# Two-block transformer kernel on one core: key tiles that hold two heads, turned queries on all partitions, four bias buffers, first scores ahead of the last values, weights ahead of the norm

## The reference, cut to what matters

```
h = rmsnorm(x) ; qa, ka, va, c_q, c_kv, k_r = split(h @ w_in)
ya = dilated attention, 8 heads of 64, with a distance bias and a mask
q  = rmsnorm(c_q) @ w_uq      -> 8 heads of 64 plain + 32 turned (rope)
kv = rmsnorm(c_kv) @ w_ukv    -> 8 heads of 64 key + 64 value; k_r turned, shared
yb = softmax((q_nope k_nope + q_rope k_rope) * 96**-0.5) @ v
x  = x + rmsnorm([rmsnorm(ya), rmsnorm(yb)] @ w_o) * norm_mix_post
x  = x + rmsnorm(conv_ffn(rmsnorm(x))) * norm_ffn_post
```

## Time and profile before

| | |
|---|---|
| median of 3 runs | 1662.87 us (1662.8 to 1668.37) |
| the profiled execution's own time | 1661.71 us |
| its span, first to last instruction | 1659.9 us |
| mean granted TensorE clock | 0.998 |
| busy: PE, DVE, ACT, POOL | 97%, 74%, 54%, 3% |
| the mixer of the first block, and its output projection | 0 to 152 us of the span |
| scores of `nat` to its first output product | 722 to 758 us |

### The profile page before, as it was taken

The page is one execution under the profiler, slowest core; times in us unless marked ns, Lnnn a source line. Parts: engine busy times, 40 slices in busy tenths (PEclk is TensorE's granted clock), DMA queues, the critical chain, the costliest instruction groups (busy, mean ns, idle before and its releaser), DMA issues.

```text
span 1659.9 us, 28581 instructions
## 1 busy us (share of the span) xinstructions
PE 1617.5 (97%) x10582; PEld 1465.1 (88%) x10582; DVE 1235.2 (74%) x1840; ACT 889.1 (54%) x1153; POOL 42.6 (3%) x54
## 2 busy tenths in 40 slices
PE   8989999999999999999999999999999999999998
PEld 7878999978799999878999999877999997899997
DVE  5765877777788777875877777447687787878787
ACT  5475545465655455565645464544554556665453
POOL 0001000000000000000000014000000000000000
PEclk9999999999999999999999999999999999999999
DMA  7252554544364544431554545543555454345543
GB/s 284 97 196 101 205 199 167 192 155 184 108 248 177 202 175 158 175 127 52 190 198 169 191 162 203 203 152 110 191 193 201 164 191 178 106 174 185 195 177 126
DMA packets 41697, 284.65 MB, mean 171 GB/s; under 512 B 4928, under 2 KB 5056, under 8 KB 8736
## 3 DMA queue, kind: packets, MB, share of 16 engines
q1 hardware_dynamic: 39424, 274.43, 45.2%
q0 software_dynamic: 2208, 9.32, 1.6%
HBM read 282.68 MB, written 1.05 MB: 171 GB/s over the span
## 4 chain that ended last, share of the span: by engine, by line
PE 84%; DVE 9%; ACT 3%; issue 3%; DMA 1%; DVEq 0%; SPq 0%; ACTq 0%
PE bank L1751 14%; PE bank L1753 14%; PE bank L1752 14%; PE bank L1845 8%; PE bank L1846 8%; PE bank L1847 8%; PE bank L1797 4%; PE bank L1798 4%; PE bank L1799 4%; DVE w_lo L982 2%; DVE arena L1249 1%; ACT w_hi L547 1%; PE bank L1733 1%; PE bank L1894 1%; PE bank L2140 1%
## 5 line engine op out<-in xcount | busy, mean ns | idle before, releaser
L1751 PE MATMUL bank<-h_hi,w_hi 128*128 128x256 f32 (+1 forms) x2240 | 642.2, 287 | 11.3 <-DVE w_lo L982 6.3
L1752 PE MATMUL bank<-h_hi,w_lo 128*128 128x256 f32 (+1 forms) x2240 | 636.3, 284 | 0.0
L1753 PE MATMUL bank<-h_lo,w_hi 128*128 128x256 f32 (+1 forms) x2240 | 636.3, 284 | 0.0
L1751 PEld LDWEIGHTS bank<-h_hi,w_hi 128*128 128x128 f32 x2240 | 429.4, 192 | 20.1 <-issue 9.5
L1752 PEld LDWEIGHTS bank<-h_hi,w_lo 128*128 128x128 f32 x2240 | 429.5, 192 | 4.5 <-issue 1.4
L1753 PEld LDWEIGHTS bank<-h_lo,w_hi 128*128 128x128 f32 x2240 | 429.5, 192 | 1.0
L982 DVE TENSOR_TENSOR w_lo<-raw,w_hi 128x2048 fp32r<-128x2048 f32 (+3 forms) x115 | 244.9, 2132 | 115.1 <-ACT w_hi L547 114.8
L1276 DVE TENSOR_TENSOR w_lo<-raw,w_hi 128x2048 fp32r<-128x2048 f32 x145 | 327.5, 2285 | 1.6 <-ACT w_hi L743 1.6
L731 ACT ACTIVATE arena<-arena,par 128x256 f32<-128x256 f32 x220 | 120.4, 594 | 358.9 <-DVE arena L1235 355.7
L743 ACT ACTIVATE w_hi<-raw 128x2048 fp32r<-128x2048 f32 x150 | 286.1, 1907 | 19.8 <-PE bank L1847 19.7
L547 ACT ACTIVATE w_hi<-raw 128x2048 fp32r<-128x2048 f32 (+2 forms) x110 | 194.3, 1772 | 107.4 <-PE bank L1847 39.0
(11 more groups left out here) (193 smaller groups left out, 1288.4 us busy)
## 6 DMA issues: line engine op xcount, KB each, us to landing
raw<-wstream SPq DMA_DIRECT2D x254, 1024.0 KB, 4.8
arena<-window_bias POOLq DMA_DIRECT2D x4, 768.0 KB, 6.7
arena<-dilated_bias POOLq DMA_DIRECT2D x8, 256.0 KB, 3.4
arena<-conv_rows POOLq DMA_DIRECT2D x2, 1024.0 KB, 4.9
raw<-wstream SPq DMA_DIRECT2D x4, 384.0 KB, 3.5
raw<-wstream SPq DMA_DIRECT2D x6, 256.0 KB, 3.0
x<-x_in SPq DMA_DIRECT2D x1, 1024.0 KB, 5.0
raw<-wstream SPq DMA_DIRECT2D x2, 512.0 KB, 7.2
```

Source lines behind the costliest of these rows:

```text
L1751: nc.tensor.matmul(dst, w_parts[0], x_parts[0], start=start, stop=False, **kw)
L1752: nc.tensor.matmul(dst, w_parts[1], x_parts[0], start=False, stop=False, **kw)
L1753: return nc.tensor.matmul(dst, w_parts[0], x_parts[1], start=False, stop=stop, **kw)
```

## The change

Nine things are changed:

- **Front.** `w_hi` of chunk 5 is made one step earlier, ahead of the root and the norm of the queries.
- **Queries and keys of `yb`.** Two chunks of turned rows come first (four heads a tile, cosine rows in one tile, swapped rows in the other), and DVE multiplies them on all 128 partitions, with tables that are repeated four times; four sums on 32 partitions each put them into place. Then come two chunks of plain queries and two of keys, a tile holding two heads, each copied by ACT in four pieces of 64 x 256. There are two chunks fewer.
- **Bias buffers.** Four in place of two (two lie in `lat`, once that is read).
- **First scores.** The scores of heads 0 and 1 are made before the last two value chunks, in `mix` and in `nat`.
- **Values.** Their last two chunks go to banks of their own; ACT copies the second half after exp(1), and PE waits for that copy before S(2,3).
- **Halves in `mix`.** ACT's at 3 and 5, 7 and 9, 10 and 12; DVE's at 5 and 6, 9 and 10, 12 and 14.
- **Halves in `nat`.** Chunk 13 is now split in attention too: ACT's halves at 2 and 3, DVE's at 3 and 4. Chunk 14: ACT's at 5 and 7, DVE's at 8 and 9.
- **`post`.** `piece * gain` first, without the root, three of four pieces beside or ahead of the root; then one instruction does `(piece * gain) * root + x`.
- **`keep_busy`** has 24 transposes in place of 36.

```
-        return [CH] * 9 + [2 * 3 * P] * 4 + [2 * 2 * P] * 4 + [2 * 256] * 2 + [CH] * 4
+        return [CH] * 9 + [2 * 3 * P] * 4 + [2 * 2 * P] * 2 + [2 * 256] * 2 + [CH] * 4
...
+                        if h == 2:
+                            pool.wait_ge(hlo_done, DT + 5)
+                        if h >= 4:
+                            pool.wait_ge(biased, bias_count(h - 4))
+                        pool.dma_start(bias_slot(h), bias_in[:, h * 512:(h + 1) * 512]).then_inc(bias_full[h % 4], 16)
...
+                    if n == 1:
+                        second_values()
...
+                            split_hi(c0 + 5)
                             inv_sqrt()
                             split_h(range(8, 11))
...
-                        2: lambda: half_hi_of(c0 + 19, 0), 3: lambda: half_hi_of(c0 + 19, 1),
-                        5: lambda: half_hi_of(c0 + 20, 0), 6: lambda: half_hi_of(c0 + 20, 1),
-                        9: lambda: half_hi_of(c0 + 21, 0), 10: lambda: half_hi_of(c0 + 21, 1),
+                        3: lambda: half_hi_of(c0 + 17, 0), 5: lambda: half_hi_of(c0 + 17, 1),
+                        7: lambda: half_hi_of(c0 + 18, 0), 9: lambda: half_hi_of(c0 + 18, 1),
+                        10: lambda: half_hi_of(c0 + 19, 0), 12: lambda: half_hi_of(c0 + 19, 1),
...
-                    attention((0, 1, 2), None, {3: lambda: half_hi_of(c0 + 14, 0), 5: lambda: half_hi_of(c0 + 14, 1)})
+                    attention((0, 1, 2), None, {2: lambda: half_hi_of(c0 + 13, 0), 3: lambda: half_hi_of(c0 + 13, 1),
+                                                5: lambda: half_hi_of(c0 + 14, 0), 7: lambda: half_hi_of(c0 + 14, 1)},
+                              second_values=lambda: value_evac(c0 + 10, v_n, heads=8, banks=banks_b, parts=(1,)))
...
+                def weighted(n):
+                    q = ORDER[n]
+                    f = q % 2
+                    dve.wait_ge(piece_sq, sq0 + n + 1)
+                    nc.vector.tensor_tensor(xs_piece(q), bank[DOWN0 + q][:, :], post_gain[:, f * 512:(f + 1) * 512], ALU.mult)\
+                             .then_inc(post_step, 1)
...
+                def add(n):
+                    q = ORDER[n]
+                    dve.wait_ge(post_step, step0 + n + 1)
+                    nc.vector.scalar_tensor_tensor(x_piece(q), xs_piece(q), tok_y[:, q // 2:q // 2 + 1], x_piece(q),
+                                                   ALU.mult, ALU.add).then_inc(x_ready, 1)
...
+                weighted(0)
+                weighted(1)
+                token_root(eps, between=lambda: weighted(2))
+                add(0)
+                add(1)
+                add(2)
+                weighted(3)
+                add(3)
...
+                    split_lo(c0 + 11)
+                    turned_products(0)
+                    split_lo(c0 + 12)
+                    turned_products(1)
+                    split_lo(c0 + 13)
+                    turned_sums(0)
+                    split_lo(c0 + 14)
+                    turned_sums(1)
+                    split_lo(c0 + 15)
+                    split_lo(c0 + 16)
...
-                                  4: lambda: half_lo_of(c0 + 19, 0), 5: lambda: half_lo_of(c0 + 19, 1),
-                                  7: lambda: half_lo_of(c0 + 20, 0), 8: lambda: half_lo_of(c0 + 20, 1),
-                                  11: lambda: half_lo_of(c0 + 21, 0), 12: lambda: half_lo_of(c0 + 21, 1),
+                                  5: lambda: half_lo_of(c0 + 17, 0), 6: lambda: half_lo_of(c0 + 17, 1),
+                                  9: lambda: half_lo_of(c0 + 18, 0), 10: lambda: half_lo_of(c0 + 18, 1),
+                                  12: lambda: half_lo_of(c0 + 19, 0), 14: lambda: half_lo_of(c0 + 19, 1),
...
-                              (0, 1, 2), None, {7: lambda: half_lo_of(c0 + 14, 0), 8: lambda: half_lo_of(c0 + 14, 1)})
+                              (0, 1, 2), None, {3: lambda: half_lo_of(c0 + 13, 0), 4: lambda: half_lo_of(c0 + 13, 1),
+                                                8: lambda: half_lo_of(c0 + 14, 0), 9: lambda: half_lo_of(c0 + 14, 1)})
...
-                    keep_busy(36, bank[7])
+                    keep_busy(24, bank[7])
...
+                    pe.wait_ge(evac_done, e0 + 5)
+                    score_pair(mix_scores, k["heads"])
+                    for c in (15, 16):
+                        token_chunk(c0 + c, c == 16, 11, 1, banks=value_banks(name, 15))
```

More of the change, by code:

```diff
@@ L247, in build_program @@
         raw_full = [sem(f"raw_full{i}") for i in range(RING)]
-        bias_full = [sem(f"bias_full{i}") for i in range(2)]
+        bias_full = [sem(f"bias_full{i}") for i in range(4)]
         tables_loaded = sem("tables_loaded")
@@ L595, in evac, with value_evac @@
                 k["evac"] += 1
-            def value_evac(c, dst, scaled=True, heads=None, func=ACT.Copy):
-                for j in range(2):
+            def value_evac(c, dst, scaled=True, heads=None, func=ACT.Copy, banks=None, parts=(0, 1)):
+                for j in parts:
                     if j == 0:
@@ L667, in post, with attention @@
                 token_root()
-            def attention(turned_groups, gain, extra, dve_copies=()):
+            def attention(turned_groups, gain, extra, dve_copies=(), second_values=None):
                 g0 = k["heads"]
@@ L782, in _ @@
                     k["ev"] += 7
[L783 to L792, removed]
+                    for c in range(9, 15):
+                        split_hi(c0 + c + 2)
+                        if c >= 11:
+                            dst, src = (q_b, k_b)[c // 13], bank[(c0 + c) % 3]
+                            act.wait_ge(chunk_used, c0 + c + 1)
+                            for i in range(4):
+                                h = 4 * ((c - 11) % 2) + i
+                                ins = nc.scalar.activation(dst[0:64, h, :], src[64 * (i % 2):64 * (i % 2) + 64, (i // 2) * S:(i // 2 + 1) * S],
+                                                           ACT.Copy, scale=(1.0, SCALE_B)[c // 13])
+                            ins.then_inc(evac_done, 1)
+                            k["evac"] += 1
@@ L809, in _ @@
                                                  scale=pcol("out_norm_b", 2 * n + t)).then_inc(hhi_done, 1)
-                    for c in range(21, 23):
+                    for c in range(19, 21):
                         split_hi(c0 + c + 2)
-                    post(c0 + 22)
+                    post(c0 + 20)
                 elif name.startswith("ffn"):
@@ L1056, in token_root @@
                 k["psq"] += 4
+                if between:
+                    between()
                 dve.wait_ge(piece_sq, k["psq"])
@@ L1415, in _ @@
                     k["wide"] += 2
-                    for c in range(20, 23):
+                    for c in range(18, 21):
                         split_lo(c0 + c + 2)
@@ L1564, in _ @@
                     eps_row = rs_row[:, :].unsqueeze(1).broadcast_to([P, 2, S])
-                    for c in range(12):
+                    for c in range(11):
                         if c:
@@ L1857, in out_chunks, with score_pair @@
                                free if i == 0 else None, between.get(i))
+            def score_pair(scores, g):
+                g0 = k["heads"]
+                for e in (g, g + 1):
+                    if e >= 2:
+                        pe.wait_ge(*((biased, bias_count(e - 2)) if has_bias(e - 2) else (exp_done, e - 1)))
+                for j in range(2):
+                    for e in (g, g + 1):
+                        q, key = scores(e - g0, j)
+                        ins = nc.tensor.matmul(bank[e % 2][:, j * S:(j + 1) * S], q, key, start=True, stop=True)
+                        if j:
+                            ins.then_inc(score_done, 1)
             def attention(scores, values, turned_groups):
@@ L2233, in pack_weights @@
             halves_of_rows(w, span(2 * 512, 512))
-            head = np.concatenate([np.arange(NOPE + ROPE), NOPE + swap])
-            for c in range(4):
-                tiles(a["w_uq"][0], *[(NOPE + ROPE) * h + head for h in (2 * c, 2 * c + 1)])
-            for c in range(4):
-                tiles(a["w_ukv"][0], *[span(P * h) for h in (2 * c, 2 * c + 1)])
+            for c in range(2):
+                turned = [np.concatenate([(NOPE + ROPE) * h + NOPE + part for h in range(4 * c, 4 * c + 4)])
+                          for part in (np.arange(ROPE), swap)]
+                tiles(a["w_uq"][0], *turned)
+            for w, width, n_chunks in ((a["w_uq"][0], NOPE + ROPE, 2), (a["w_ukv"][0], P, 2)):
+                pairs = [np.concatenate([span(width * h, NOPE), span(width * (h + 1), NOPE)]) for h in range(0, HB, 2)]
+                for c in range(n_chunks):
+                    tiles(w, pairs[2 * c], pairs[2 * c + 1])
             values = np.concatenate([span(P * h + 64, 64) for h in range(HB)])
```

153 lines of the change are left out of this document (73 added, 80 removed).

## The result

The changed kernel takes **1675.64 us** (median of 11 runs, 1669.18 to 1681.54) against 1663.57 us for the kernel before (11 runs, 1661.99 to 1668.37): ratio **1.0067**, interval [1.0055, 1.0079]. The forecast was 1663.4, range 1654.0 to 1668.5. The time lies above the range, and by the 0.5% bound the kernel is slower, which had 0.04.

A forecast was written before the change was run, and what follows sets the result against it. PE, busy 97% of the span, was taken to bound the kernel. Terms 1.7 - 1.8 - 2.9 + 3.5 = +0.5 on the profiled 1661.71, with the median 1.2 above, gave 1663.4 us; range 1654 to 1668.5.

The forecast's parts named there:

- The addition of the waits: In both attentions: instruction times summed along the queues, putting the first output product 1.7 later in `mix`, 3.5 in `nat`.
- the low clock taken for it: At S(2,3) of `mix`: low clock assumed as before, so S(2,3) at 87.1 and V(0) at 90.9.
- the forecast case: Whole kernel: the main forecast, 1663.4 us, with 1660.5 to 1666 given a chance of 0.45.
- six new waits: In the two attentions: six holes of 1 to 2.7 us, listed beside one of 3.4.
- rival 2: In the new holes of both attentions and behind `ffn0`: the clock falls, giving 1669.2 us; chance 0.12.
- Three more where PE has no slack: In the attentions: three further low-clock episodes at some 1.6 us each, 4.8 us in all.
- I take it to stay up: Behind `ffn0`, turning of x: gap falls from 2.25 to 1.6, the clock stays full, 1.0 us more gained.
- The term of -2.9: Behind `ffn0`: 1.9 us gained by the new norm order plus 1.0 by the clock staying up.
- Rival 1: In `mix` and `nat`: the halves cost little, as ACT is ahead or PE's backlog covers; 1653.7 us; chance 0.15.
- rival 3: Second value copy behind exp(1) holds PE, table load with drain: `mix` +4, `nat` +5, 1667 us; chance 0.08.
- Rival 4: Only the norm part counts; the halves cancel the lead in `mix` and `nat`: 1659.9 us; chance 0.20.

The follow-up runs named there:

- filled: The changed kernel, its late halves kept, with 123 transposes into unread columns ahead of the waits of its two attentions; 1665.01 us, ratio 1.0004.
- after: The changed kernel itself, with all nine changes, against the kernel before; 1675.64 us, ratio 1.0067.
- norm-only kernel: The kernel before with only the new `post` and 24 transposes in place of 36; 1659.59 us, ratio 0.9980.
- halves back: The changed kernel with the halves of `mix` and `nat` where they stood before; 1657.71 us, and 1653.63 us with 30 transposes ahead of S(2,3) of `mix`.
- DVE's halves one step later: The changed kernel with only DVE's halves in `mix` moved, to heads 6 and 7, 10 and 11, 13 and 14; 1664.42 us, ratio 0.9995.
- the front as before: The changed kernel with old halves, 30 transposes in `mix`'s hole, 14 in `nat`'s, and chunk 5's split back behind the root; 1652.95 us, ratio 0.9927.

## Why the prediction was wrong

Two rows of PE's timeline of the kernel before complete the comparison, the first products behind `mix`'s norm and behind `ffn0`'s:

```profile
159.92 0.36 PE L1751 MATMUL bank<-h_hi,w_hi 128*128 128x256 f32 x1
...
358.24 0.69 PE L1797 MATMUL bank<-w_hi,h_hi 128*128 128x512 f32 x1
```

Each column is the change against before of one stretch of the profiled execution, between the starts of these products (filled: 130.67 - 129.17 = +1.5, and so on).

| stretch | forecast | attentions' waits filled | after |
|---|---|---|---|
| to the first output product of `mix` | +1.7 | +1.5 | +5.7 |
| to the product behind `mix`'s norm | -1.8 | -1.6 | -1.6 |
| to the product behind `ffn0`'s norm | -2.9 | -2.5 | -1.9 |
| to the first output product of `nat` | +3.5 | +3.4 | +5.0 |
| to the end of the span | 0 | +0.1 | -0.1 |
| sum | +0.5 | +0.9 | +7.1 |

- **The addition of the waits was right.** At full clock every stretch is within 0.4 us of its forecast, and the profiled execution (1662.91) within 0.7 of the 1662.2 forecast for it. In after S(0,1) started at 80.34, S(2,3) at 87.96, V(0) at 90.37 and T(6) at 102.52, where 79.9, 87.1, 90.9 and 102.8 were written; PE waited 1.37 for S(8) and 2.14 for V(11), where 1.6 and 2.2 were. The front lost 0.54 (50.68 against 50.14), where 0.5 was. Behind `mix`'s last product the 24 transposes end at 160.41, 0.7 ahead of x, as the prediction had it. DVE's idle time for ACT's half was 3.4 (head 5), 4.2 (head 12) and 4.0 (`nat`), as forecast; at head 9 it was 4.1 in after, at low clock, but 1.3 in the filled kernel, where DVE had waited 2.6 for the turned outputs just before. One agreement is luck: S(2,3) came 0.9 later than forecast, and the low clock taken for it and what follows did not come, so V(0) followed it after 2.4 us and not 3.8. The two errors leave 0.5.
- **The step that failed** is the clock left out of the forecast case, at nothing for six new waits, and with it rival 2's price. With the clock at 0.999 or more the same waits gave 1665.01, with the clock falling behind them 1675.64: the term was worth 10.6 us in the median, the low clock behind `ffn0` (next point) included. "Three more where PE has no slack", at "some 1.6 us" each, took the size of an episode from 355 to 359 us, a turning of x followed by large products. In attention the low stretch was 14 us, and the same code had 4, 9 and 13 in three traces. The forecast case took its nothing from one row: behind 1.65 at 724.84 the scores took 1.13. Behind 1.65 at 727.16 in after they do so again (1.14). But the norm-only kernel, which has `nat` and its wait of 1.65 as before, took 2.08 for these scores:

```profile
720.85 2.08 PE L1886 MATMUL bank<-arena 64*128 64x256 f32 x8 [1.65 <-DVE arena L1173]
```

```profile
720.00:724.00 4.00, 3.15 (x14) 2.42 (x15) 2.64 (x7) 1.70 (x4) 0.00 (x0) 0.58 0.12 47
```

  So one execution at full clock behind a wait was no evidence that the wait is harmless.
- **Behind `ffn0`** "I take it to stay up" was wrong in after: the gap shrank from 2.25 to 1.71, and the clock fell all the same behind it and the 0.96 that follows: the two halves of x took 1.09 and 1.77. In the norm-only and the filled kernels the same gaps (1.71, 0.96) left it at 1.00. The term of -2.9 measured -1.9 in after and -2.5 in the filled kernel.
- **The median** was taken 1.2 above the profiled execution, as before. After, it is 6.5 above. The runs of one kernel follow their clock: 1669.18 us at 0.993, 1675.64 at 0.987, 1681.54 at 0.985 (others lie up to 3.3 us off such a line); with the waits filled all are at 0.999 or 1.0, within 3.3 us.
- **Rival 1** did not come true because DVE's waits were real; **rival 3** fell with the table load, between which and exp nothing stood. **Rival 4** had +1.7 for the two attentions together, and the filled kernel has +1.5 and +3.4. **Rival 2** had the direction and the mechanism, and 1669.2 was exactly the best of the eleven runs, by chance: it is 6.4 below their median. Its 0.12 was too small: the trace of before had two low stretches at waits (1.47 and 2.25) and one exception (1.65).

The Trainium skill (TensorE: Matmul & The Clock Gate, Part 1) says that the throttled clock is the default and that activity releases it. The filled kernel agrees: the same schedule with transposes in its waits ran at 1.00 where after had 0.51.

## What to carry to other kernels

In a stage where PE waits often and briefly, work out the waits, then price the clock beside them: half of PE's time over whatever stretch of attention follows, 4 to 14 us here, and more in the median run than in one lucky profile. Where a split's first half on ACT and its partner on DVE stand at the same step of an in-order list, move the partner one step later before anything else. A wait that can't be taken away can be filled with products that nobody reads, as long as they are shorter than the wait: that moved nothing by more than 0.12 us where it was compared, and the medians fell by 4.1 us with one hole filled (halves back) and by 10.6 with those of both attentions, a part of which, in the traces, lies where nothing was filled. With the late halves, filling only the longest hole was no clear gain.

## What the runs showed that was not expected

- The length of a low stretch varies between traces of the same code behind the same wait: 4, 9 and 13 us behind 2.52 us in `nat`.
- The longest wait isn't the one that the clock falls behind: in after the clock stays at 1.00 behind 3.49 us (S(2,3) takes 1.13) and falls 15 us later behind 1.37 and 1.00; with both halves back it falls behind 3.51 in the same place (2.08), and with DVE's halves one step later it falls about 1 us after S(2,3) has started. Behind the same two gaps at `ffn0` (1.71 and 0.96) it stayed low for some 3 us in after and 6 with the front as before, and did not fall in the norm-only and filled kernels. What decides was not tested.
- A low clock hides waits: in after it swallowed those at S(12) and V(9), since PE was too slow to arrive early. From T(6) to the first output product 8.6 us of lost clock (one minus the clock, 103 to 131) made 4.1 us of time (32.4 us against 28.3 with every wait filled).
